# A two-block transformer kernel: a merged opening, attention in pairs of heads, a head norm over rows and a merged end

## The reference, cut to what matters

```python
def first_block(x, mem, ...):
    u = rmsnorm(x, g_mix); qa, ka, va, qb, kb, vb = jnp.split(u @ w_in, 6, axis=-1)
    ya = dilated_attention(...)   # windows (128,1), (512,4), (2048,16), merged by their log-sum-exp
    yb = moba_attention(...)      # at 256 tokens: causal attention with a bucketed bias
    h = x + concat(rmsnorm(ya), rmsnorm(yb)) @ w_out
    h = h + memory_cross_attention(rmsnorm(h), rmsnorm(mem))
    h = h + conv_ffn(rmsnorm(h))
    return rmsnorm(h, g_final)

def _neighbourhood_attention(q, k, v, kc, vc, rpb):   # 8 heads, 4 rows of 64 latent tokens
    s = concat(where(col_mask, q @ k + bias(rpb), -inf), q @ kc)   # window keys and context keys
    p = softmax(s); return p_win @ v + p_ctx @ vc
def _context_attention(q, k, v): ...                  # context queries, layer 0 only

def _head_norm(y, g, b):          # one group per head of 64
    mu = mean(y, -1); var = mean(square(y - mu), -1)
    return (y - mu) * rsqrt(var + 64e-5) * g + b
# per direction: out += (_head_norm(y) + bonus) * gate; in layer 1 only latent tokens are needed
# the very end: _rmsnorm(xl, final_g), mean of squares over the 1024 channels of a token
```

## Time and profile before

| | |
|---|---|
| Median of 3 runs | 3601.2 us (3599.58 to 3604.52) |
| Profiled execution, own time | 3604.86 us |
| Its span in the trace | 3603.1 us |
| PE busy | 3285.3 us (91%) |
| DVE, ACT, POOL busy | 1041.6 (29%), 462.0 (13%), 181.7 (5%) |
| Read from HBM | 557 MB |
| Mean granted clock of PE | 0.948 |

### The profile page before, as it was taken

The page is one execution under the profiler, slowest core; times in us unless marked ns, Lnnn a source line. Parts: engine busy times, 40 slices in busy tenths (PEclk is TensorE's granted clock), DMA queues, the critical chain, the costliest instruction groups (busy, mean ns, idle before and its releaser), DMA issues. The chain is left out here.

```text
span 3603.1 us, 37049 instructions
## 1 busy us (share of the span) xinstructions
PE 3285.3 (91%) x15201; PEld 1877.7 (52%) x15201; DVE 1041.6 (29%) x2036; ACT 462.0 (13%) x947; POOL 181.7 (5%) x225
## 2 busy tenths in 40 slices
PE   4988999979898789999979886699999999999998
PEld 3665788834457434444444475444444444444444
DVE  2236477536544532210037345300000000000001
ACT  0120100023132110000023221200000100000000
POOL 1000000000003200000000142000000000000000
PEclk9999999989879899999999898799999999999998
DMA  5315366611300033312222200198989888888984
GB/s 167 118 39 203 133 234 210 210 63 61 81 1 3 1 105 118 128 48 75 76 74 87 56 3 2 62 326 276 294 274 297 270 274 295 275 296 273 296 272 147
DMA packets 293206, 560.50 MB, mean 156 GB/s; under 512 B 29447, under 2 KB 42403, under 8 KB 293073
## 3 DMA queue, kind: packets, MB, share of 16 engines
q1 hardware_dynamic: 271959, 500.47, 42.5%
q0 software_dynamic: 13792, 50.52, 3.9%
q10 hardware_dynamic: 7322, 7.62, 0.8%
HBM read 557.36 MB, written 1.23 MB: 155 GB/s over the span
## 5 line engine op out<-in xcount | busy, mean ns | idle before, releaser
L1148 PE MATMUL bank<-normed,weight_ring 128*128 128x256 f32 (+1 forms) x2240 | 680.1, 466 | 73.9 <-PEq L1864 43.3
L1148 PEld LDWEIGHTS bank<-normed,weight_ring 128*128 128x128 f32 x2240 | 434.8, 195 | 312.6 <-issue 273.4
L2313 PE MATMUL bank<-weight_ring,work 128*128 128x512 f32 x1024 | 449.4, 593 | 10.1 <-ACT work L2346 10.1
L2313 PE MATMUL bank<-work 128*128 128x512 f32 x768 | 337.5, 592 | 0.0
L2313 PEld LDWEIGHTS bank<-weight_ring,work 128*128 128x128 f32 x1024 | 192.0, 190 | 241.1 <-issue 241.1
L654 PE MATMUL bank<-normed,weight_ring 128*128 128x512 f32 (+1 forms) x704 | 282.5, 562 | 24.7 <-PEq L1258 24.7
L1148 PE MATMUL bank<-work,weight_ring 128*128 128x256 f32 (+1 forms) x896 | 283.5, 477 | 9.2 <-PEq L1124 9.2
L2367 DVE TENSOR_TENSOR work<-bank,work 128x512 f32<-128x512 f32 x56 | 38.7, 692 | 787.8 <-PE bank L2313 787.8
L215 DVE SCALAR_TENSOR_TENSOR work<-work,small 128x512 f32<-128x512 f32 x336 | 237.6, 749 | 15.0 <-DMA work<-in_mod_w 7.9
L2313 PEld LDWEIGHTS bank<-work 128*128 128x128 f32 x768 | 144.7, 190 | 176.0 <-issue 176.0
L1148 PEld LDWEIGHTS bank<-work,weight_ring 128*128 128x128 f32 x896 | 172.4, 193 | 116.6 <-issue 102.9
(11 more groups left out here) (303 smaller groups left out, 2749.0 us busy)
## 6 DMA issues: line engine op xcount, KB each, us to landing
weight_ring<-in_moe_w_gate SPq DMA_DIRECT2D x64, 1024.0 KB, 5.1
weight_ring<-in_moe_w_up SPq DMA_DIRECT2D x64, 1024.0 KB, 5.1
weight_ring<-in_moe_w_down SPq DMA_DIRECT2D x64, 1024.0 KB, 5.1
work<-in_mod_w POOLq DMA_DIRECT2D x48, 1024.0 KB, 6.8
work<-in_moe_w_gate SPq DMA_DIRECT2D x48, 1024.0 KB, 5.1
work<-in_moe_w_up SPq DMA_DIRECT2D x48, 1024.0 KB, 5.1
work<-in_moe_w_down SPq DMA_DIRECT2D x48, 1024.0 KB, 5.0
weight_ring<-in_w_in SPq DMA_DIRECT2D x36, 1024.0 KB, 5.2
```

The costliest lines, as they stand in the source:

```text
L1148: last = nc.tensor.matmul(banks(gi)[j][:, 0:a.shape[-1]], w[:, k, j * P:(j + 1) * P], a, start=k0 + k == 0, stop=k0 + k == total - 1)
L2313: last = nc.tensor.matmul(self.bank[b], xg[:, kk], w[:, k], start=kk == 0, stop=kk == DT - 1)
```

## The change

1. **One opening block** (`opening`) in place of five. x is loaded first, its two halves by two queues, 26 merged vector loads follow on SyncE and ACT, weights after them, and tables, mem and ctx by POOL. The norm is taken while tokens lie on partitions: ACT squares and sums, the reciprocal root goes into a diagonal matrix, and x times that diagonal turns and scales at once. The bias lines and the conditions are made in the same block.
2. **Attention in pairs of heads** (`head_attention`) for block one and both layers of block two. Scores of two heads lie in two banks and use the two row halves, the value products the two column halves. One DVE instruction adds the bias and takes the minimum of the negated sum; ACT exponentiates from SBUF. No flip: the queries are stored reversed in runs of 128 or 64 and the result is moved out reversed. Context keys get their bias from a tile of zeros beside the bias. The multiplicity is a logarithm in the bias table.
3. **Head norm** over rows, heads' sums by DVE reductions, transposes behind the scaling, gain and offset by ACT, and only latent tokens in layer 1.
4. **End**: the final norm joins `store`, behind the transposes; its gain comes as a broadcast tile, loaded in the experts' first block.
5. The arena hands out `sh`, `ld`, `cvout` and others in another order.

```diff
-        m[N_BUCKETS, :] = ~seen
+        m[N_BUCKETS, :] = np.where(seen, np.log(np.maximum(weight, 1)) / NEG, 1.0)
...
+    def head_attention(self, pairs, bias_in=None):
...
+        pr = self.arena.take("pr", 6, keys)
+        pt = self.arena.take("pt", 4, keys)
...
+        S, PT, O = self.bank[0:4], self.bank[4:6], self.bank[6:8]
...
+                def scores(p):
+                    u = pairs[p]
+                    if p >= 2:
+                        free = biased if pairs[p - 2]["bias"] else expd
+                        pe.wait_ge(free.sem, free.at(2 * (p - 1)))
+                    for h in range(2):
+                        nc.tensor.matmul(S[2 * (p % 2) + h][:, 0:u["keys"]], u["q"][h], u["k"][h], start=True, stop=True).then_inc(scored.sem, 1)
...
+                    for t in range(nkt):
+                        for h in range(2):
+                            last = nc.tensor.matmul(O[p % 2][h * HD:(h + 1) * HD, 0:P], u["v"][h][t], pt[:, (2 * p + h) % 4, t * P:(t + 1) * P],
+                                                    start=t == 0, stop=t == nkt - 1)
...
+                            nc.vector.tensor_tensor_reduce(parts(pr[:, i % 6, 0:u["keys"]]), parts(s), u["bias"][h], -1.0, -NEG, ALU.add, ALU.min, low).then_inc(biased.sem, 1)
+                        else:
...
+                            nc.vector.tensor_reduce(low, s, AX_X, ALU.max, negate=True).then_inc(biased.sem, 1)
...
-                if bias_in:
-                    pe.wait_ge(shaped.sem, shaped.at(32))
...
-                        last = nc.tensor.matmul(S[i % 3][:, nk - u["bias"].shape[-1]:nk], flip, u["bias"], start=False, stop=True)
...
+    def opening(self, specs, memT):
...
+                sync.dma_start(tok[:, 0, 0], ins["x"][0, 0:P, :]).then_inc(xin.sem, 16)
...
+                self.load_weights(sync, 0)
...
+                for i, name in ((1, "mem"), (2, "ctx_2")):
+                    pool.dma_start(tok[:, i], ins[name][0].rearrange("(t p) d -> p t d", p=P)).then_inc(win.sem, 16)
...
+                            last = nc.tensor.matmul(self.bank[4 + 2 * t + b][:, k * P:(k + 1) * P], tok[:, 0, t, c], diag[:, t], start=True, stop=True)
...
+                for d in range(2):
+                    nc.vector.tensor_reduce(sums[:, d, 0], heads(rows[d]), AX_X, ALU.add).then_inc(mean.sem, 1)
...
+                    nc.vector.reciprocal(sums[:, d, 1], sums[:, d, 1]).then_inc(var.sem, 1)
...
-                    nc.vector.reciprocal(yT[:, i], yT[:, i]).then_inc(st.sem, 1)
...
-        self.rmsnorm(lambda k: xT[:, k, LAT], DT, SEQ, [(slice(0, SEQ), lambda k: xT[:, k, LAT], lambda k: self.col("final_g", k), None)])
...
+        self.load([(final_gain, bass.AP(ins["final_g_2"].tensor, 0, [[0, P], [1, D]])), (router, ins["moe_router_2"][0].rearrange("(k p) e -> p k e", p=P)),
...
+                        nc.scalar.activation(dump[:, 2 * t + b], self.bank[2 * t + b], ACT.Square, accum_out=st[:, t, b:b + 1]).then_inc(squared.sem, 1)
```

More of the change, by code:

```diff
@@ L171, in free, with span @@
             del self.used[n]
+    def span(self, one, other, at, n):
+        a, b = self.used[one][0], self.used[other][0] + at
+        return bass.AP(self.tensor, a, [[self.size, P], [b - a, 2], [1, n]])
 class SideProduct:
@@ L1310, in attention @@
+    def attention(self, units):
         nc = self.nc
@@ L1601, in copy_f @@
[L1601 removed]
+    def copy_f(self, dst, j0, sl=BOTH, scale=None, run=None):
         def fn(eng, banks):
@@ new lines, in _ @@
+                for i in range(4):
+                    act.wait_ge(turned.sem, turned.at(i + 1))
+                    nc.scalar.activation(o[:, i], self.bank[i][:, 0:nt * P], ACT.Identity, bias=self.col(f"gn_b{layer}", i % 2),
+                                         scale=self.col(f"gn_g{layer}", i % 2)).then_inc(gained.sem, 1)
+        for q, k in ((mean, 4), (centred, 2), (squared, 2), (var, 6), (rooted, 2), (normed, 2), (turned, 4), (gained, 4), (summed, 4)):
+            q.advance(k)
+        ar.free("sq", "head_sums", "o")
@@ L2005, in block_two @@
-            for hd in range(8):
-                a, ft = (hd % 2) * HD, hd // 2
-                for i in range(2):
-                    tq = slice(SEQ + i * P, SEQ + (i + 1) * P)
-                    units.append(dict(q=[qk[a:a + HD, ft, tq]], k=[qk[a:a + HD, 4 + ft, :]], head=hd,
-                                      v=[v[:, t, hd * HD:(hd + 1) * HD] for t in range(4)],
-                                      out=[hT[a:a + HD, ft, tq]], out_part=a, bias=bias[:, hd, i], count=None))
-            self.attention(units, flip, bias_in)
@@ L2013, in block_two @@
-            ar.free("qk", "v", "bias", "window", "flip")
+            bias_in = dict(heads=heads, zero=unbiased, shape=(window, self.table_src("window")))
+            pairs = []
+            for seen, keys in ((CTX, CTX), (LAT, BOTH)):
+                if seen == CTX and not ctx:
+                    continue
+                for n in range(4):
+                    for i in range(2):
+                        tq = slice(seen.start + i * P, seen.start + (i + 1) * P)
+                        pairs.append(dict(q=[qk[a:a + HD, n, tq] for a in (0, HD)], k=[qk[a:a + HD, 4 + n, keys] for a in (0, HD)], head=2 * n,
+                                          v=[[v[:, t, hd * HD:(hd + 1) * HD] for t in range(keys.stop // P)] for hd in (2 * n, 2 * n + 1)],
+                                          out=hT[:, n, tq], bias=[ar.span("unbiased", "bias", (2 * hd + i) * SEQ, SEQ) for hd in (2 * n, 2 * n + 1)] if seen == LAT else None,
+                                          keys=keys.stop, run=GRID_W))
```

710 lines of the change are left out of this document (417 added, 293 removed).

## The result

The changed kernel takes 3391.3 us (median of 4 runs, 3388.5 to 3398.2) against 3602.9 for the kernel before beside it: ratio 0.9416, 95% interval 0.9399 to 0.9433. The profiled execution took 3390.67 us.

A forecast was written before the change was run, and what follows sets the result against it. TensorE was taken to carry the kernel, VectorE the head norm. Savings 41 + 25 + 28 + 14 + 37 + 9.4 - 1.4 = 153 from 3604.9 gave 3452, less 3.7 for the median: 3448 us, range 3405 to 3495.

The forecast's parts named there:

- Block one's attention: Attention of block one: 16 pairs at 2.4 us plus 3, 41.4 against 66.4 us, 25 us saved.
- 2 x (0.50 + 0.16 + 0.35) + 0.29 = 2.31: Block one's attention: VectorE's time in us for one pair of heads.
- scores between 0.85 and 1.24: Block one's attention: TensorE's us for a pair's scores, 0.85 if packed on array halves, 1.24 if not.
- 2.2 per pair: Bound for block one's attention: a pair at 2.2 us, which would save 28 us.
- no packing: Array halves don't overlap: 3.16 us per block-one pair on TensorE, 13 us saved there; as a rival 3504 us, chance 0.06.
- Layer 0's attention: Neighbourhood attention of layer 0: 76 us against 103.8, 28 us saved, starting at the low clock.
- I take it to rise after three latent pairs: Layer 0's attention: clock low for eight context pairs and three latent pairs, high for the other five.
- high from the start: Rival: full clock from the start of the neighbourhood attentions, as TensorE skips the window-table wait; 34 us more saved, 3414, chance 0.12.
- stays low: Rival: clock low through both neighbourhood attentions, 18 + 19 us less saved, 3485 us, chance 0.13.
- Layer 1's attention: Neighbourhood attention of layer 1: 2.5 pairs low, 5.5 high, ending at 2066.7 against 2080.8, 14 us saved.
- So 2025.3: Layer 1's attention: time in us when POOL finishes the second head's bias, which the first pair needs.
- The slow new instruction: Rival: VectorE's fused add-and-minimum at the reciprocal's pace costs 125 us more, 3573; chance 0.05, of which 0.02 slower than before.

The follow-up runs named there:

- the two-query pairs: The changed kernel with each pair made of the two query tiles of one head, not two heads, so both members share array halves: 3439.6 us.

## Why the prediction was right or wrong

**What bounds the kernel now**: right as read. The low clock of layer 0 was seen in the earlier trace rows and its length worked out (66 us); what was not seen is that it went on for 26 us into the latent units.

**Opening, head norm, end, gain load**: right, term by term (37.9 and 1.1 for 41; 15.2 and 22.6 for 37, though TensorE's wait around the norm is 19.3 and 12.3 for 17 and 10; 9.8 for 9.4; -1.2 for -1.4). They were sums of durations along a chain in which each step waits for the last, and there a duration is what counts.

**Block one's attention**, 35.6 saved for 25: the mechanism was right, the size was off, in the sum "2 x (0.50 + 0.16 + 0.35) + 0.29 = 2.31" and in "scores between 0.85 and 1.24". In a stream of instructions that don't wait for each other the price of one is the distance from start to start, not its duration: the fused one 0.34 where the trace prints 0.42, its read nothing where I added 0.08. The earlier trace rows had shown it: rows of 0.70 and 0.38 that start 0.54 and 0.31 apart. I used distances for the flip product (0.54), the transposes (2 x 0.31) and the unpacked scores (2 x 0.62), and durations for the value products (0.66, measured 0.59) and for all of VectorE. The 0.85 for packed scores has no working; they take 0.63, and the earlier trace rows, with 0.72 for as many columns, was nearer. 16 pairs x 0.6 = 9.6 of the 10.6 us. The bounds "2.2 per pair" and "no packing" (3.16, where the two-query pairs take 2.66) didn't hold the truth: both were too long in the same way. Packing is as the earlier trace rows said, and the rival without it is refuted by the two-query pairs.

**Layer 0's attention**, 58.0 for 28: two steps failed. The unit prices again (3.11 us for a 512-key pair where I had 3.7, 1.81 and at 1.2 GHz 3.25 for a context pair where I had 2.4 and 4.2), and "I take it to rise after three latent pairs". With the measured prices and my clock the stage would be 8 x 3.25 + 3 x 6.2 + 5 x 3.1 + 2 = 62 us, so 14 of the 29 us between 76 and 47 are prices and 15 the clock. The clock step had no row behind it: in the kernel before the clock rose 26 us into the latent units, and that was carried over to pairs that are another stream of products, under which it came back after 7 us. The rival "high from the start" gave 3414, the nearest of the cases, and was wrong in its reason: the clock does start low, with the wait there or not, and comes back under the pairs, by a property that was not found. The rival "stays low" is refuted for the pairs.

**Layer 1's attention**, 25.7 for 14: 3.1 instead of 3.7 for each of eight pairs gives 5 us; the rest is mostly the clock, low for 5.75 us behind the wait where two and a half pairs, 18 us, were forecast. "So 2025.3" for the second head's bias was right in kind: TensorE waits for it, 6.63 us.

**What I left unpriced**, the wait for the window table, is 2 us ahead of each layer by the run that puts it back, and nothing on balance in layer 1, where the bias is waited for anyway. The other 2 and 3 us of the long stretches between are within what two executions of one kernel differ by.

**The slow new instruction** never came: 418 and 686 ns.

**The range** was built from the clock cases and from bounds that shared one mistake. An error of a tenth to a quarter in every attention term goes the same way three times, and the range had no room for that.

## What to carry to other kernels

Price an instruction in a gapless stream by the distance to the next start, and keep durations for chains that wait; a bound made of durations is no lower bound. Before costing a stage that runs at the low clock, ask whether the stream itself keeps it there, and whether the change makes it another stream. Where two engines tie, say what each is worth on its own: cutting VectorE's part brought nothing in block one, and lengthening it was paid in full.

## What the runs showed of the hardware

The granted clock stayed at 0.50 for 47 us under a TensorE that was busy without a gap, on products one head at a time. With one 128x128 product more in each context unit it was 1.00 for 90 us when entered high, and 0.50 for 75 us when entered low.

POOL's additions and VectorE's scalings get in each other's way. In layer 1 of the changed kernel, while POOL adds the window:

```profile
1875.63 0.49 DVE L1370 TENSOR_SCALAR work<-work 128x512 f32<-128x512 f32 x1
1876.22 1.30 DVE L1370 TENSOR_SCALAR work<-work 128x512 f32<-128x512 f32 x1
...
1875.72 1.52 POOL L1299 TENSOR_TENSOR work<-work 128x512 f32<-128x512 f32 x1 [1.04 <-DMA work<-rpb_lines]
```

The scaling from SBUF to SBUF takes 0.49 us when it starts ahead of POOL's addition, which then takes 1.52 instead of 1.26, and 1.30 when the addition (1875.72 to 1877.24) is under way. The Trainium skill (SBUF — State Buffer, SBUF: two separate sides) says that the port pair which VectorE and GpSimd share is an exclusive lock held for a whole instruction; the trace agrees, whoever starts first is served first, and the second scaling ends 0.28 us behind POOL's addition. The two scalings of 1.3 us ahead of the fall of the clock in layer 0 are of the same kind: they start 0.07 and 0.09 us behind an addition (898.61 and 900.04).
